# The gate piece of each inversion level moves from the first filler slot to the second

## What is computed

```
def rwkv_scan(r, w, k, v, kk, b, s0, reverse):       # for each of two directions
    sa = einsum('bhvk,bhk->bhv', s, kk_t)
    s = s * w_t - sa[..., None] * b_t + v_t[..., None] * k_t
    y = einsum('bhvk,bhk->bhv', s, r_t)
softmax(q k^T * scale + bias) v                      # attention, per head and 128 queries
gates = sigmoid(zg);  zg = h @ w_in[:, gate columns]
```

## Time and profile before

| | |
|---|---|
| median of 3 timed runs | 2193.54 us (2191.72 to 2200.48) |
| the profiled execution | 2188.24 us, of which the span on the engines is 2186.5 us |
| PE busy over the span | 1930.8 us, 88% |
| DVE, ACT, POOL busy | 1017.9, 494.0, 693.0 us |
| granted TensorE clock, mean | 0.947 of full speed |
| stretch with the ten units | from about 610 to 1280 us of the span |

### The profile page before, as it was taken

The page is one execution under the profiler, slowest core; times in us unless marked ns, Lnnn a source line. Parts: engine busy times, 40 slices in busy tenths (PEclk is TensorE's granted clock), DMA queues, the critical chain, the costliest instruction groups (busy, mean ns, idle before and its releaser), DMA issues. The chain is left out here.

```text
span 2186.5 us, 40476 instructions
## 1 busy us (share of the span) xinstructions
PE 1930.8 (88%) x15900; PEld 1417.7 (65%) x15900; DVE 1017.9 (47%) x2087; ACT 494.0 (23%) x933; POOL 693.0 (32%) x1036
## 2 busy tenths in 40 slices
PE   7999999897689999999999965998799999999956
PEld 2565655465467777777777745954477888878722
DVE  3868666476345444545344442645712222222246
ACT  2111222110233233333333311201122122212100
POOL 4526000000043323433233222322234444444425
PEclk9999999999899999999999977999899999999978
DMA  8234656552241222102120027630199999999773
GB/s 277 58 130 139 222 194 219 179 202 82 63 127 28 64 62 62 50 28 68 46 64 16 7 60 269 214 121 29 52 371 340 328 302 316 338 335 341 261 305 139
DMA packets 227216, 355.65 MB, mean 163 GB/s; under 512 B 38177, under 2 KB 156724, under 8 KB 223236
## 3 DMA queue, kind: packets, MB, share of 16 engines
q1 hardware_dynamic: 200206, 300.47, 40.6%
q0 software_dynamic: 24560, 45.27, 5.9%
q10 hardware_dynamic: 2310, 7.92, 1.0%
HBM read 307.11 MB, written 84.34 MB: 179 GB/s over the span
## 5 line engine op out<-in xcount | busy, mean ns | idle before, releaser
L2815 DVE TENSOR_TENSOR me_hh<-me_sg,ps_ju 128x128 f32<-128x128 f32 x76 | 21.9, 288 | 386.2 <-PE ps_jd L2767 369.7
L452 PE MATMUL ps_s<-hT,w_in_sb 128*128 128x512 f32 x432 | 194.8, 604 | 0.0
L2759 PE MATMUL ps_jg<-me_xT,me_wg 128*128 128x128 f32 x1216 | 149.2, 276 | 0.0
L1343 PE MATMUL ps_gs<-hT,gt_w 128*128 128x512 f32 x256 | 142.3, 638 | 7.3 <-PEq L76 7.3
L2759 PE MATMUL ps_ju<-me_xT,me_wu 128*128 128x128 f32 x1216 | 148.2, 275 | 0.0
L2767 PE MATMUL ps_jd<-me_wd,me_hh 128*128 128x512 f32 x304 | 143.1, 593 | 2.4 <-DVE me_yb L2821 2.4
L2759 PEld LDWEIGHTS ps_jg<-me_xT,me_wg 128*128 128x128 f32 x1216 | 142.9, 193 | 0.0
L452 PEld LDWEIGHTS ps_s<-hT,w_in_sb 128*128 128x128 f32 x432 | 81.7, 194 | 93.5 <-issue 92.9
L2759 PEld LDWEIGHTS ps_ju<-me_xT,me_wu 128*128 128x128 f32 x1216 | 141.9, 192 | 0.0
L2038 POOL TENSOR_TENSOR rc_lj<-rc_l,rc_lev 128x256 f32<-128x256 f32 x100 | 74.3, 762 | 178.7 <-PE ps_c L1730 178.3
L2788 ACT ACTIVATE me_xT<-ps_jx 128x1024 f32<-128x1024 f32 x77 | 78.9, 1025 | 209.8 <-PE ps_jx L2750 209.8
(11 more groups left out here) (548 smaller groups left out, 3954.3 us busy)
## 6 DMA issues: line engine op xcount, KB each, us to landing
me_wg<-in_exp_w_gate SPq DMA_DIRECT2D x76, 512.0 KB
me_wu<-in_exp_w_up SPq DMA_DIRECT2D x76, 512.0 KB
me_wd<-in_exp_w_down SPq DMA_DIRECT2D x76, 512.0 KB
cb_rows<-yj_dram SPq DMA_DIRECT2D x10, 2048.0 KB
w_ad_sb<-in_w_ada SPq DMA_DIRECT2D x32, 512.0 KB
w_in_sb<-in_w_in SPq DMA_DIRECT2D x31, 512.0 KB
gt_w<-in_w_in SPq DMA_DIRECT2D x24, 512.0 KB, 4.4
zr<-in_w_ada SPq DMA_DIRECT2D x4, 2048.0 KB, 8.8
```

What stands on the lines that cost most here:

```text
L452: mm(ps_s[:, b, :], w_in[:, r, k, :], hT[:, k, 0:TS], start=(k == 0), stop=(k == KT - 1))
L1343: nc.tensor.matmul(ps_s[:], w[:, t % WR, k, :], hT[:, k, 0:TS], start=(k == 0), stop=(k == KT - 1))
L2759: last = mm(o[:, 0:P], w[:, s, k, :], xT[:, s % 2, k, :], start=(k == 0), stop=(k == KT - 1))
```

## The change

The two letters of the slots are exchanged. The order of a level becomes P1, **A**, P2, **G, A**. It holds on every engine for levels 0 to 4 of all ten units, on SP too, where the M pieces of all five levels and then the first four L pieces stand together ahead of the loads of the unit after the next. No instruction is added or removed, and no buffer or size is changed.

```
-FILL_GRAM, FILL_LAST, FILL_TURNED, FILL_MID, FILL_LEVEL = "GA", "G", "AG", "GA", "A"
+FILL_GRAM, FILL_LAST, FILL_TURNED, FILL_MID, FILL_LEVEL = "GA", "G", "AG", "A", "GA"
```

## The result

The changed kernel takes 2209.77 us (median of 5 runs, 2206.25 to 2211.6) against 2193.54. The ratio is 1.0069, 95% interval 1.0049 to 1.0089: 0.7% slower, 16 us. The forecast was 2214 us, with a range of 2201 to 2225.

What follows compares the result with a forecast made beforehand. PE, busy 88% of the span and running in program order, was taken as the bound. Waits 11.5 plus clock 4.2 and 4.8 gave 20.5 us, added to the median 2193.5: 2214 us, 0.9% slower, range 2201 to 2225.

Steps and rivals of the forecast that it cites:

- PE's order and the two gaps: Levels: M-to-L gap grows by a G, 0.78 us wait goes; L-to-M gap shrinks, wait 0.43 becomes 1.70, +1.27.
- Level 0: DVE's scans fix when level 1's M piece can start; PE arrives a G earlier, V's waits reach 3.3 to 4.9 us.
- The sum of the waits: PE's waits over the ten units: +11.5 us, −11 from waits that go and +22.5 from waits that grow.
- the shift of DVE's block: Units 2, 4, 6, 8: P2 of level 0 comes 1.2 us earlier; block's shift put at 0, between −1.2 and +0.5 per unit.
- The clock: PE at half clock behind waits: +4.2 us for units 1, 4, 7 and +4.8 us for new waits of 1.70.
- The guess that four of six new waits of 1.71 would cost a fall: Units 1, 3 to 7: four clock drops from 1.00 to 0.50 at 1.2 us each, +4.8 us.
- the prediction's prices: Clock loss per fall: about 1.4 us behind each long wait of units 1, 4, 7; 1.2 us behind a 1.70 wait.
- The other queues: ACT's moved sigmoid, SP's weight loads and POOL's later `lj` have cover or slack; no term in the sum.
- The one of no change: Nothing to measure, chance 0.20: DVE's block ends 1.2 us earlier in units 2, 4, 6, 8, no short-wait falls; 9 us, 2202.
- The faster one: Chance 0.05: scans freed from overlap all last 1.36 us, eight units regain about 2 us each, fewer falls; 2181 us.

Runs made afterwards that it cites:

- levels 2 to 4 alone: The kernel before with the new slots in levels 2 to 4 only, levels 0 and 1 as before; ratio 1.0001 (0.9983 to 1.0020).
- the placement by kind alone: The kernel before with each unit's five G's placed by kind of attention piece, two ahead of the piece behind the scans; 2172.62 us, ratio 0.9918.

## Why the prediction held

**PE's order and the two gaps.** Right. L and P1 come one G later, M and P2 do not; T follows S by the same 2.86 us; 0.78 in L is gone in levels 2 to 4 where it was said to go (in level 4 of unit 6 it is what is left of 1.51, as forecast), and 1.71 stands in each M that was named.

**Level 0.** Right in kind and place: the G of level 1 lost its use because the scans end when they end. The experiments show it from three sides: the G put back, the scans moved, the scans shortened.

**The sum of the waits** was forecast at +11.5 us, and is +8.5 (39.6 to 48.1). By units, forecast and measured: 0: −1.25 and −1.1; 1: +2.9 and +3.4; 2: +0.6 and −0.5; 3: +0.5 and −0.5; 4: +1.8 and +1.4; 5: +2.9 and +2.9; 6: +0.5 and +0.1; 7: +2.9 and +3.1; 8: +0.6 and −0.2; 9: 0 and 0. The term that was mis-sized is the shift of DVE's block (the four scans and two subtractions), put at 0. In units 2, 4, 6 and 8, where P2 of level 0 comes earlier by a G, the block started 1.1 to 1.3 us earlier, took 0.2 to 0.7 us longer, and so ended 0.5 to 0.8 us earlier; the scans of unit 4 took 2.54 us where the earlier trace rows has 1.36. In unit 3 the wait of 1.0 behind the scans vanished, as the four scans took 1.74 us instead of 3.44; in unit 1 they took 3.91 instead of 2.72. In units 1 and 3 the block starts where it did, and what differs is how long POOL's instructions run beside the scans.

**The clock** was forecast at +9.0, and PE's working time grew by 8.4. That these agree is in part luck. The guess that four of six new waits of 1.71 would cost a fall was met exactly (those of units 1, 4, 6 and 7; not 3 and 5), but with levels 2 to 4 alone only two of the six did, and the working time stayed as it was. Units 1, 4 and 7, with two new falls each, lost 10.1 us (3.7, 2.5 and 3.9), where the prediction's prices give 7.8. Unit 6 lost nothing: its fall behind a wait of 1.85 us in the kernel before went as the new one came. Units 2 and 5 got 2.3 us back, which the forecast had not. And the clock falls in level 1 of six units, not of seven or eight: in unit 3 no wait was left there, and in unit 6 none followed the 1.43 us.

**The other queues.** Right that SP and the gate weights don't show: PE waits for no weights in the level part. Wrong in one respect: the sigmoid does hold up ACT's copy in L of level 0, by 0.7 us in unit 1. In the changed kernel it was hidden behind the longer wait for DVE, and showed only when that was gone.

**The rivals.** The one of no change had the right mechanism in its first half, the earlier block, but at half its size, and not without the clock's falls. The argument against it, that the earlier scans would be stretched by as much by POOL, held only in part: they won those 0.5 to 0.8 us. The faster one (all scans 1.36) needed POOL out of the way; when I moved most of it out, the changed kernel lost its deficit (1.0016, interval 0.9999 to 1.0033), but didn't become faster than the kernel before, as that rival had it. What the move would give the kernel before, no run shows.

## What to carry to other kernels

Filler hides a wait only if it stands between the producer's end and the waiting instruction, so count for each wait what lies in that gap; a fixed pattern that meets a cycle of three kinds of pieces suits no kind of unit well, and a table by kind was worth 0.8% here. Look at what stands ahead of the producer in its own queue before moving filler: putting 4 to 5 us of unhurried DVE work behind an urgent copy was worth as much, and made the question of the slot void. And a wait of TensorE can cost more than its length: here the six of 2.8 us and more were each followed by the lower clock, and filling one of them gave back 2.3 us. Whether a wait of 1.7 us costs that too can't be told beforehand, so a term for it belongs in the range rather than in the sum.

## What the hardware showed that I had not expected

A wait of 1.71 us was followed by the clock of 1.2 GHz in five of eight places of the changed kernel and not in three, with the same kinds of instructions around it. The place alone doesn't decide it. Ahead of the bonus product of unit 3, PE waits 1.99 or 2.00 us in all twelve traces, behind 20 us in which it stood still for nothing else and ran the same products. The granted clock in the 4 us behind that wait was 0.60 in the kernel before, 0.57 in the changed one with the scans moved, about 0.8 in four others and 1.00 in six. Nor is every longer wait followed by a fall: with the placement by kind alone PE waited 2.94 us in unit 5, behind two G's of which one is double, and the clock was 1.00 in the 13 us behind it:

```profile
956.95 0.66 PE L1506 MATMUL ps_ax<-ident,at_p 128*128 128x128 f32 x4 [2.94 <-ACT at_p L1592]
```

What decides is open, and it differs between executions of the same program part, so one trace doesn't give a wait's price.

And four DVE scans of 128 columns, 1.36 us by themselves, took up to 4.2 us while POOL worked on SBUF: something that trebles the time of an instruction, and of which no wait in the profile tells.
